# Gate product with high and low weights as one stationary operand, and chunk states on alternating row halves

## The reference

```python
h = rms_norm(x, norm1_g)
proj = h @ w_in                                   # ga: 16 of its columns
gate_pre = ga @ gla_gate_w2 + gla_gate_b          # (256, 16) @ (16, 512)
log_g = log_sigmoid(gate_pre) / 16
# chunks of C = 64 positions, n = 0..3, per head; b = cumsum(log_g) in a chunk
k_dec = kc * exp(b_last - b)
chunk_state = einsum('bhncd,bhncv->bhndv', k_dec, vc)     # contraction over the 64 positions
# scan: o_n = q_n @ state; state = decay_n * state + chunk_state_n
```

## Time and profile before

| | us |
|---|---|
| median of 3 runs | 1972.41 (1971.65 to 1972.62) |
| profiled execution | 1971.09 |
| its span, first to last instruction | 1969.3 |
| PE busy | 1946.4 (99%) |
| PEld (weight loads) busy | 1600.0 (81%) |
| DVE busy | 1095.9 (56%) |
| ACT busy | 939.1 (48%) |
| POOL busy | 108.5 (6%) |

### The profile page before, as it was taken

One profiled execution on the slowest core, in us unless ns is written; L12 is line 12 of the kernel. 1 busy time (PEld: TensorE's weight loads), 2 busy tenths in 40 slices (PEclk: granted clock), 3 DMA queues, 4 the chain that ended last, 5 costly groups with the idle time before them and its releaser, 6 DMA issues.

```text
span 1969.3 us, 22692 instructions
## 1 busy us (share of the span) xinstructions
PE 1946.4 (99%) x9062; PEld 1600.0 (81%) x9062; DVE 1095.9 (56%) x1330; ACT 939.1 (48%) x1230; POOL 108.5 (6%) x326
## 2 busy tenths in 40 slices
PE   8999999999999999999999999999999999999998
PEld 6788887788888888888888888888888888787787
DVE  4556455664545545445445556544655665666674
ACT  6445354554444344443444554444444464655653
POOL 1111000200000000000000010001100003001100
PEclk9999999999999999999999999999999999999999
DMA  7566564466665666665666566665566655544445
GB/s 238 175 193 171 152 173 159 154 179 192 186 192 190 193 193 190 187 189 193 193 190 191 182 193 183 192 193 171 168 184 189 192 179 176 150 150 141 138 149 161
DMA packets 182441, 352.74 MB, mean 179 GB/s; under 512 B 11136, under 2 KB 11952, under 8 KB 182336
## 3 DMA queue, kind: packets, MB, share of 16 engines
q1 hardware_dynamic: 181520, 349.18, 58.3%
q0 software_dynamic: 816, 2.11, 0.7%
HBM read 349.14 MB, written 2.11 MB: 178 GB/s over the span
## 4 chain that ended last, share of the span: by engine, by line
PE 93%; DVE 3%; POOL 1%; ACT 1%; issue 1%; DMA 0%; DVEq 0%; SPq 0%; ACTq 0%
PE g L790 29%; PE g L792 29%; PE g L791 29%; PE m L755 3%; DVE wl L1225 1%; ACT TW L985 1%; DVE st L1234 1%; PE m L871 1%; DVE TW L1225 1%; ACT wh L988 0%; POOL st L1589 0%; PE ob L889 0%; PE ob L888 0%; PE ob L887 0%; PE m L862 0%
## 5 line engine op out<-in xcount | busy, mean ns | idle before, releaser
L1225 DVE TENSOR_TENSOR wl<-raw,wh 128x1024 fp32r<-128x1024 f32 x657 | 801.5, 1222 | 770.7 <-ACT wh L988 770.1
L988 ACT ACTIVATE wh<-raw 128x1024 fp32r<-128x1024 f32 x657 | 694.5, 1058 | 837.6 <-PE g L792 834.9
L790 PE MATMUL g<-wh,xh 128*128 128x512 f32 x1888 | 748.0, 396 | 2.7 <-DVE wl L1225 2.7
L792 PE MATMUL g<-wh,xl 128*128 128x512 f32 x1888 | 736.8, 390 | 0.0
L791 PE MATMUL g<-wl,xh 128*128 128x512 f32 x1888 | 735.7, 390 | 0.0
L790 PEld LDWEIGHTS g<-wh,xh 128*128 128x128 f32 x1888 | 354.8, 188 | 80.1 <-issue 5.5
L792 PEld LDWEIGHTS g<-wh,xl 128*128 128x128 f32 x1888 | 354.6, 188 | 75.2
L791 PEld LDWEIGHTS g<-wl,xh 128*128 128x128 f32 x1888 | 355.1, 188 | 70.4
L790 PE MATMUL g<-wh,mh 128*128 128x512 f32 x736 | 291.5, 396 | 0.0
L792 PE MATMUL g<-wh,ml 128*128 128x512 f32 x736 | 287.1, 390 | 0.0
L791 PE MATMUL g<-wl,mh 128*128 128x512 f32 x736 | 286.7, 390 | 0.0
(11 more groups left out here) (131 smaller groups left out, 840.4 us busy)
## 6 DMA issues: line engine op xcount, KB each, us to landing
raw<-in_ev_w_in SPq DMA_DIRECT2D x128, 512.0 KB, 3.7
raw<-in_w_in SPq DMA_DIRECT2D x96, 512.0 KB, 3.9
raw<-in_w_gate SPq DMA_DIRECT2D x88, 512.0 KB, 4.3
raw<-in_w_up SPq DMA_DIRECT2D x88, 512.0 KB, 3.7
raw<-in_w_down SPq DMA_DIRECT2D x88, 512.0 KB, 4.7
raw<-in_od_w_in SPq DMA_DIRECT2D x72, 512.0 KB, 3.6
raw<-in_w_out SPq DMA_DIRECT2D x32, 512.0 KB, 4.3
raw<-in_ev_w_out SPq DMA_DIRECT2D x32, 512.0 KB, 3.7
```

Of the source, the lines that this page charges most:

```text
L790: e.matmul(o, hi[:, kt, c], h, start=first, stop=False)
L792: last = e.matmul(o, lo[:, kt, c], h, start=False, stop=end)
L988: return e.activation(o, i, AF.Copy, scale=scale)
L1225: return e.tensor_tensor(o, a, b, op)
```

## The change

- The gate unit's high and low weights lie side by side in the `wh` slot, for each k tile 16 high and 16 low columns. PE takes these 32 as one stationary operand, with the high activations and then the low ones: two matmuls per k tile, into 32 partitions (which adds the product of low by low). `gaT`, the reciprocal norms' bank and `w2` get 32 partitions, `w2` twice the same 16 rows, loaded by two DMAs, so that "g_gate" adds the two halves by its contraction.
- `g_state` steps are listed in another order: (0,0), (1,0); then (0,1), (1,1); then (2,0), (2,1). PE does nothing at n = 0; at n = 1 it waits for both banks and makes chunks 0 and 1 of that h2, for head after head, by turns on the two halves of the rows; at n = 2 chunk 2 alone.

```diff
         say("g_decay")
-        for n in range(3):
-            for h2 in range(2):
+        for h2 in range(2):
+            for n in range(2):
                 say("g_state", n, h2)
             yield
+        for h2 in range(2):
+            say("g_state", 2, h2)
+        yield
...
-        gaT = sb("gaT", [16, 256])
-        w2 = sb("w2", [16, 512])
+        gaT = sb("gaT", [32, 256])
+        w2 = sb("w2", [32, 512])
...
+        def pair(u):
+
+            return wh[:, u % NS, 0:32 * KT].rearrange("p (k c n) -> p k c n", c=2, n=16)
...
+                        o = g2(u)[0][0:32, 0:256]
                         for kt in un.kts:
-                            h, l = (z[:, u % NS, 16 * kt:16 * kt + 16] for z in (wh, wl))
-                            o = g2(u)[0][0:16, 0:256]
-                            e.matmul(o, h, hi[:, kt, :], start=kt == 0, stop=False)
-                            e.matmul(o, l, hi[:, kt, :], start=False, stop=False)
-                            last = e.matmul(o, h, lo[:, kt, :], start=False, stop=kt == KT - 1)
+                            hl = wh[:, u % NS, 32 * kt:32 * kt + 32]
+                            e.matmul(o, hl, hi[:, kt, :], start=kt == 0, stop=False)
+                            last = e.matmul(o, hl, lo[:, kt, :], start=False, stop=kt == KT - 1)
...
-                        last = e.matmul(bank(*p)[0:16, 128 * k:128 * k + 128],
-                                        rr[:, k:k + 1].to_broadcast([128, 16]), ident, start=True, stop=True)
+                        last = e.matmul(bank(*p)[0:32, 128 * k:128 * k + 128],
+                                        rr[:, k:k + 1].to_broadcast([128, 32]), ident, start=True, stop=True)
...
-                elif kind == "g_state":
+                elif kind == "g_state" and a[0] > 0:
                     n, h2 = a
-                    k, lo = n // 2, 64 * (n % 2)
-                    on.wait_ge(*moved("g_kturn", k))
+                    chunks = (0, 1) if n == 1 else (2,)
+                    on.wait_ge(*moved("g_kturn", n // 2))
                     on.wait_ge(*taken(bi[("va", 1)]))
-                    on.wait_ge(*bank_free(*p))
+                    for c in chunks:
+                        on.wait_ge(*bank_free("g_state", c, h2))
                     for i in range(2):
                         h = 2 * h2 + i
-                        last = e.matmul(bank(*p)[:, 256 * i:256 * i + 256], kd[lo:lo + 64, k, h, :],
-                                        va[lo:lo + 64, k, 256 * h:256 * h + 256], start=True, stop=True)
-                    last.then_inc(s_bank, 1)
+                        for c in chunks:
+                            k, lo = c // 2, 64 * (c % 2)
+                            last = e.matmul(bank("g_state", c, h2)[:, 256 * i:256 * i + 256], kd[lo:lo + 64, k, h, :],
+                                            va[lo:lo + 64, k, 256 * h:256 * h + 256], start=True, stop=True)
+                            if i == 1:
+                                last.then_inc(s_bank, 1)
...
-                    copy(wh[:, u % NS, 0:m], raw[:, u % NR, 0:m]).then_inc(s_hi, 1)
+                    if units[u].block.n == 16:
+                        copy(pair(u)[:, :, 0, :], raw[:, u % NR, 0:m].rearrange("p (k n) -> p k n", n=16)).then_inc(s_hi, 1)
+                    else:
+                        copy(wh[:, u % NS, 0:m], raw[:, u % NR, 0:m]).then_inc(s_hi, 1)
...
-                    tt(wl[:, u % NS, 0:m], raw[:, u % NR, 0:m], wh[:, u % NS, 0:m].bitcast(f32),
-                       ALU.subtract).then_inc(s_lo, 1)
+                    if units[u].block.n == 16:
+                        tt(pair(u)[:, :, 1, :], raw[:, u % NR, 0:m].rearrange("p (k n) -> p k n", n=16),
+                           pair(u)[:, :, 0, :].bitcast(f32), ALU.subtract).then_inc(s_lo, 1)
+                    else:
+                        tt(wl[:, u % NS, 0:m], raw[:, u % NR, 0:m], wh[:, u % NS, 0:m].bitcast(f32),
+                           ALU.subtract).then_inc(s_lo, 1)
...
-            e.dma_start(w2[:, :], t["w2"]).then_inc(s_w2, 16)
+            for i in range(2):
+                e.dma_start(w2[16 * i:16 * i + 16, :], t["w2"]).then_inc(s_w2, 16)
```

More of the change, by code:

```diff
@@ L891, in tensor @@
                     on.wait_ge(*moved(*find("gates")))
-                    on.wait_ge(s_w2, 16)
+                    on.wait_ge(s_w2, 32)
                     on.wait_ge(*bank_free(*p))
@@ L1075, in scalar @@
                     on.wait_ge(*product(a[-1]))
-                    copy(gaT[:, :], banks(a[-1])[0][0:16, 0:256]).then_inc(s_read_act, 1)
+                    copy(gaT[:, :], banks(a[-1])[0][0:32, 0:256]).then_inc(s_read_act, 1)
                 elif kind == "sr":
@@ L1314, in vector @@
                     on.wait_ge(*taken(a[-1]))
-                    tt(gaT[:, :], gaT[:, :], bank(*p)[0:16, 0:256], ALU.mult).then_inc(s_bank_dve, 1)
+                    tt(gaT[:, :], gaT[:, :], bank(*p)[0:32, 0:256], ALU.mult).then_inc(s_bank_dve, 1)
                 elif kind == "bias":
```

## The result

The changed kernel takes 1968.07 us (median of 17 runs, 1967.45 to 1969.17), the one before, in the same comparison, 1972.19 (17 runs, 1971.46 to 1972.98). The ratio is 0.998, 95% interval 0.9973 to 0.9986. That is 4.12 us or 0.21%, just over the 0.2% that I had called about what a measurement can tell from no change; 1968.8 was forecast, 1967.6 to 1971.0 the range. Of the 0.7 us between forecast and result, 0.2 lie in the base: the forecast was taken off 1972.41, the median of three runs.

A forecast was written before the change was run, and what follows sets the result against it. The prediction took PE to bound the kernel: 1.88 us from the gate block plus 1.72 from the chunk states, 3.60 in all, off the median 1972.41 gave 1968.8 us, range 1967.6 to 1971.0.

The forecast's parts named there:

- What bounds it: Whole kernel: PE busy 1946.4 of 1969.3 us, so a microsecond taken from PE comes off the end.
- Gates: Gate block on PE: 32 matmuls instead of 48 at an unchanged 0.1173 us each, saving 1.88 us, bound 2.00.
- more than forecast: Rival: gate matmuls step by 0.1135 us and both paired state groups halve entirely, 3.92 us saved, 1968.5; chance 0.10.
- States: Chunk states on PE: two paired groups take 1.06 us instead of 1.92 each, saving 1.72 us, bounds 0 to 1.92.
- entry and exit: Chunk-state groups on PE: 0.10 us going in and 0.10 going out per group, still three groups, so no change.
- The drain rival: Two mixed state groups: each change of row half costs 0.19 us, unpaired, 2.66 lost against 1.88 saved, 1973.2; chance 0.04.
- Covers: Side effects of the change on banks, gate split, evacuation and start-up DMA, each costed at nothing because slack hides it.
- the banks: Second state group on PE: DVE frees its bank by about 322.3, needed at 324.2 or later, margin 1.9 us.
- the split: Gate unit's split on ACT and DVE: shorter runs, ready by 209.6, used at 213.88, so 4.3 us cover any doubling.
- SP's margin: Start-up on SP's queue: the second small DMA ends 0.2 us before the next weight load; cost 0, bounds 0 to 0.64.
- The chances: Whole kernel, measured against 0.2%: faster 0.30, within 0.68, slower 0.02.

## Why the prediction was right, and where it wasn't

- *What bounds it.* Right. 3.69 us off PE came off the end: 3.7 us behind the gate block's start in the traces, and 4.12, 3.83 and 3.56 as medians of three comparisons, additive in the parts.
- *Gates.* The term was 1.88, with 2.00 as bound; it measured 1.98. The step that failed is "a gain per matmul has no reason: the moved columns are the same 256". The step fell to 0.114, from the fifth matmul on right at the value I had as the best one, and the run with sixteen columns shows that it goes with the number of stationary columns. This part of "more than forecast" came true. The Trainium skill, "TensorE: Matmul & The Clock Gate", section "Back-to-back issue gap", gives 262 cycles for 256 columns, an estimate of 0.109 us, as the gap of a matmul by itself; neither kernel's stream met it.
- *States.* 1.72 forecast, 1.71 measured, with entry and exit unchanged. Reading it from L862 and L864, another layer with the same form, was exact. The reason given, turns between neighbours, was too narrow: half after half pairs as well without them, so the order of neighbours in L862 and L864 was not the reason to rely on.
- *The drain rival* fell: a change of half within a group costs nothing. But the price for going in and out is real. I put it at 0.20 inside a group and 0.09 ahead of it; with the longer step behind the group it is nearer 0.4. I counted it correctly as unchanged for the states, and did not ask what it would bring to remove it where it can be: 1.2 us at the gates, a third of the change's own gain.
- *Covers.* Those of the banks and of the split held. DVE's copy for the bank ran 320.21 to 320.90, and PE's second group began at 323.05, 2.15 us later (1.9 forecast). The gate unit was split by 210.1, 4.3 us ahead of its use, and the unit after the gates in time. SP's margin, forecast at 0.2 us, was 0.25, 0.38 and none at all in three traces of the same kernel: a margin as thin as this is no cover, and it was luck that the 0.1 us by which the load came late did not show at the end.
- *The chances.* The gain as PE's rows give it is 0.19%, and the three comparisons lie on both sides of 0.2%: 0.209%, 0.194% and 0.181%. That the first lies beyond it is scatter, about 0.4 us that no PE row shows; 0.30 for faster allowed for that.

## What to carry to other kernels

Where PE is the bound, two f32 matmuls with 64 rows on opposite halves cost what one costs, if they stand in one group; the order inside does not matter. Two products that share an operand are better made with the others side by side in the stationary one while it is narrow, as the count of matmuls is what costs. A small f32 group on 32 or 64 rows between full matmuls pays about 0.4 us for going in and out, and one on 32 stationary columns about 0.3: fill it up with zeros to the whole array when nothing can run beside it. And when a change is as small as a kernel's scatter, measure the stretch of the trace from the change on: here three traces of one kernel agreed within 0.1 us in it, where their spans lay 0.9 apart.

## What was not expected of the hardware

- With 256 columns moved, rounded matmuls with 32 stationary columns step by 0.114 us (0.1136 after the first four) and with 16 by 0.117.
- Rounded matmuls with 32 stationary columns go in and out between full ones without a price (0.23 and 0.12 us), while f32 ones with 32 pay 0.28.
- PE starts the second half's matmuls beside the first half's although two of the first half stand ahead of them in the program (1.07 us for eight passes in either order).
- Four f32 column tiles of 32 columns run together: eight passes in 0.43 us.
- In the start-up the step for 512 columns falls from 0.43 to 0.23 us at a time that differs from execution to execution, with its last long step beginning between 10.7 and 14.4 us, while the granted clock reads 1.00 before and after it; it alone moved the profiled spans by 0.47 us.
